# Down matrices of the experts issued from ScalarE's DMA queue in a two-layer decoder step

## The reference, cut to what matters

```python
def expert_block(args):
    xblk, e = args
    hid = jax.nn.silu(xblk @ w_eg[e]) * (xblk @ w_eu[e])
    return hid @ w_ed[e]
```

## Time and profile before

| | us |
|---|---|
| median of 3 runs | 1869.09 |
| lowest and highest | 1864.49, 1871.01 |
| the profiled execution, its own time | 1871.93 |
| its span in the profile | 1870.2 |
| PE busy | 1424.5 |
| DVE busy | 473.6 |
| ACT busy | 323.3 |
| POOL busy | 299.8 |

### The profile page before, as it was taken

How to read it: one execution, slowest core, us unless ns; L and a number is a source line. 1 busy time by engine, 2 the same in 40 slices (tenths; PEclk the granted TensorE clock), 3 DMA queues, 4 the chain that set the end, 5 groups by cost and what they waited for, 6 DMA issues and landing times. The chain is left out here.

```text
span 1870.2 us, 20816 instructions
## 1 busy us (share of the span) xinstructions
PE 1424.5 (76%) x7932; PEld 780.5 (42%) x7932; DVE 473.6 (25%) x1019; ACT 323.3 (17%) x656; POOL 299.8 (16%) x394
## 2 busy tenths in 40 slices
PE   6999655599498777777771799878599877777770
PEld 3554233445254444444440443345355444444440
DVE  1013544532411000000003287822411100000014
ACT  3122221201111000000001143544111000000001
POOL 1000010100111111111110285700012111111110
PEclk9999655598699999999996799978699999999995
DMA  7600000113799999999994800410599999999984
GB/s 210 242 25 1 6 1 3 18 23 45 326 418 419 420 421 420 420 420 420 420 391 153 295 0 1 180 19 12 221 395 418 420 420 420 420 420 420 420 365 156
DMA packets 99025, 478.04 MB, mean 256 GB/s; under 512 B 25463, under 2 KB 28551, under 8 KB 49784
## 3 DMA queue, kind: packets, MB, share of 16 engines
q1 hardware_dynamic: 86040, 452.67, 59.8%
q0 software_dynamic: 12928, 24.62, 4.7%
HBM read 467.50 MB, written 28.27 MB: 265 GB/s over the span
## 5 line engine op out<-in xcount | busy, mean ns | idle before, releaser
L1312 PE MATMUL psum<-ring,arena 128*64 128x256 f32 x4096 | 470.4, 384 | 99.5 <-DMA ring<-in_w_expert_up 57.9
L1312 PEld LDWEIGHTS psum<-ring,arena 128*64 128x64 f32 x4096 | 293.3, 138 | 259.1 <-DMA ring<-in_w_expert_up 79.7
L1333 PE MATMUL psum<-ring,arena 128*64 128x512 f32 x1024 | 238.9, 608 | 77.3 <-issue 75.6
L1436 POOL COPY arena<-arena 128x1 int32 (+1 forms) x122 | 23.2, 190 | 854.2 <-DVE arena L1414 646.1
L1333 PEld LDWEIGHTS psum<-ring,arena 128*64 128x64 f32 x1024 | 79.7, 139 | 192.0 <-issue 188.4
L1414 DVE COPY arena<-psum 128x512 f32<-128x512 f32 x64 | 44.3, 692 | 325.9 <-PE psum L1333 325.9
L1889 PE MATMUL psum<-arena,ring 128*128 128x512 f32 x256 | 114.2, 605 | 8.7 <-DMA ring<-in_w_pw 8.7
L2122 DVE SCALAR_TENSOR_TENSOR psum<-arena,psum 128x512 f32<-128x512 f32 x136 | 102.8, 756 | 16.1 <-PE psum L1903 11.6
L1405 DVE TENSOR_TENSOR arena<-psum,arena 128x256 f32<-128x256 f32 x64 | 27.2, 425 | 306.2 <-ACT arena L1377 306.2
L1830 POOL TENSOR_TENSOR ring<-ring 128x512 f32<-128x512 f32 x72 | 91.6, 1273 | 39.3 <-ACT ring L2024 24.3
L1371 ACT ACTIVATE arena<-psum 128x512 f32<-128x512 f32 x64 | 38.2, 597 | 323.7 <-PE psum L1299 323.7
(11 more groups left out here) (398 smaller groups left out, 1270.0 us busy)
## 6 DMA issues: line engine op xcount, KB each, us to landing
ring<-in_w_expert_gate SPq DMA_DIRECT2D x64, 2048.0 KB, 34.2
ring<-in_w_expert_up SPq DMA_DIRECT2D x64, 2048.0 KB, 34.4
ring<-in_w_expert_down SPq DMA_DIRECT2D x64, 2048.0 KB, 34.5
arena<-y_rows SPq DMA_DIRECT2D x16, 512.0 KB, 6.4
ring<-in_w_pw SPq DMA_DIRECT2D x4, 2048.0 KB, 21.1
ring<-in_w_in_mix SPq DMA_DIRECT2D x3, 2048.0 KB, 20.4
ring<-in_w_out_mix SPq DMA_DIRECT2D x1, 4096.0 KB, 29.1
ring<-in_w_pw SPq DMA_DIRECT2D x1, 4096.0 KB, 25.8
```

The source lines that it names most:

```text
L1312: last = nc.tensor.matmul(P[q * CAP:(q + 1) * CAP, bank, 0:HF], Q["xt"][:, c, h, :], w[:, h, c, q * HF:(q + 1) * HF], start=(h == 0 and c ...
L1333: last = nc.tensor.matmul(P[q * CAP:(q + 1) * CAP, 4, :], Q["hidt"][:, c, h, :], ring(u)[2][:, h, c, q * HB:(q + 1) * HB], start=(h == 0 a ...
```

## The change

SP no longer issues the down matrices of the experts 3 to 31. ACT issues them: behind the copy of turned hidden rows of expert `e` it waits for `y_done` of expert `e - 1` and issues down(e+2). The last round of three experts is taken out of ACT's loop, since the expert 30 has no matrix to issue. Gate and up stay with SP, in their order. The same is done in both layers, and in the code of further passes, which isn't run for these inputs.

```diff
             def sp_rest(self, sp, layer, before):
 
-                def step(e, u):
-                    self.load(sp, layer, e, u, before, True, (0, 1))
-                    self.load(sp, layer, e - 1, (u + 2) % 3, before, True, (2,))
-
                 self.load(sp, layer, 3, 0, before, True, (0, 1))
                 with sp.Fori(0, (NE - 5) // 3) as i:
                     for c in range(3):
-                        step(i * 3 + (4 + c), (1 + c) % 3)
-                step(NE - 1, (NE - 1) % 3)
-                self.load(sp, layer, NE - 1, (NE - 1) % 3, before, True, (2,))
-
+                        self.load(sp, layer, i * 3 + (4 + c), (1 + c) % 3, before, True, (0, 1))
+                self.load(sp, layer, NE - 1, (NE - 1) % 3, before, True, (0, 1))
...
-            def act(self, act, before):
+            def act(self, act, layer, before):
...
                         sigmoid(e)
                         copy_x(e + 1)
                         copy_hid(e)
+                        if isinstance(e, int) and e + 2 >= NE:
+                            continue
+                        self.load(act, layer, e + 2, c, before, True, (2,))
 
                 three(0)
-                with act.Fori(1, (NE - 2) // 3) as i:
+                with act.Fori(1, (NE - 2) // 3 - 1) as i:
                     three(i)
+                three((NE - 2) // 3 - 1)
                 sigmoid(NE - 1)
                 copy_hid(NE - 1)
```

More of the change, by code:

```diff
@@ L1581, in moe_act @@
                 nc.scalar.activation(VAL[:, 1, :, :, 0], Q["oh2"], ACT.Copy, scale=Q["m5"][:, 10, 0:1]).then_inc(RE["vals_made"], 1)
-                main_pass.act(act, 0)
-                more(act, layer, lambda b: more_pass.act(act, b))
+                main_pass.act(act, layer, 0)
+                more(act, layer, lambda b: more_pass.act(act, layer, b))
                 if final:
```

## The result

The changed kernel takes 1888.91 us (median of 5 runs, 1883.37 to 1892.37) against 1871.01 (5 runs, 1864.49 to 1874.81): a ratio of 1.0096, 95% interval 1.0068 to 1.0124. It is slower by 17.9 us; 17.0 were forecast. The profiled execution has a span of 1887.2 us, 17.0 us more than before.

A forecast was written before the change was run, and what follows sets the result against it. The prediction took the DMA engines, full at 420 GB/s, to bound both expert passes. PE's tail after the last landing grows 8.5 us a layer: 1869.1 + 17.0 = 1886.1 us, range 1868 to 1900.

The forecast's parts named there:

- The stream bounds the pass and keeps its length: Both expert passes: busy DMA engines limit them; first issue to last landing stays 461 us in layer 1, at 420 GB/s.
- Nothing is won on SP, nothing lost on ACT: Issue of weights: 29 x 4.31 us a layer saved on SP worth nothing; ACT's added issues covered, 0 us.
- A down matrix shares the engines instead of standing behind SP's backlog: Down loads from ACT's queue: landing about 13 us after issue instead of 34.5.
- Down(31) lands about 9 us before up(31): End of each pass: down(31), issued about 22 us before the end, lands 13 us later; up(31) lands last.
- The tail grows by 8.5 us a layer, 17.0 in all: PE's work after the last landing: 3.60 + 4.91 us more in each layer; chance 0.66.
- the 4.91 us: End of layer 1 on PE: time from start of down(30) to start of down(31), turn and copy included.
- the lower end: Tail after the last landing: 0.4 us may be a wait for down(31), so 8.1 us a layer, 16.2 in all.
- The order of landing stays: Rival, end of pass: down(31) still lands last, tail stays 3.65 us, time 1869 to 1871 us; chance 0.13.
- Faster: Rival, DMA engines: second queue raises the rate; 2.5%, 431 GB/s, would give 1863 us; chance 0.07.
- slower still: Rival, DMA engines: interleaving two queues costs rate, adding 11 to 22 us, 1897 to 1908 us; chance 0.14.

The follow-up runs named there:

- e2: Changed kernel, but down(30) and down(31) issued by SP behind up(31), ACT issuing down only up to expert 29: 1872.04 us against 1867.95 for the kernel before.
- e4: Kernel before, but ACT issues the gate matrices, SP up and down in their old order: 1876.99 us, ratio 1.0043 to the kernel before.
- e1: Kernel before, SP issuing everything, but down(30) and down(31) ahead of gate(31) and up(31): 1888.03 us against 1867.95.
- e6: Kernel with SP issuing down(30), down(31) ahead of gate(31), up(31), plus 56 unused small matmuls ahead of gate(31): 1886.94 us; kernel before 1867.89.

## Why the prediction was right

*The stream bounds the pass and keeps its length.* Right: 460.3 to 461.9 us in layer 1 and 472.0 to 473.2 in layer 0, in all eight kernels, with one queue or two.

*Nothing is won on SP, nothing lost on ACT.* Right: a gate's issue on SP fell from 4.45 to 0.37 us in the median without a gain. ACT's took 0.38 us, and e2 bounds all costs of the second queue at 6.5 us.

*A down matrix shares the engines instead of standing behind SP's backlog.* Right, with 14.8 us in the steady stretch where 13 was worked out. The Trainium skill (DMA: Bandwidth & Descriptors, section Queues, rings and completion order) has a ring for ACT on every engine, served in turn; the new queue q10 and the 14.9 us beside 40 agree. What the Trainium skill says on the same page, section Issuing engines are not separate DMA queues, that issuing from several engines only saves issue time, agrees with the rate here, 420 GB/s both times; the order of landing changed all the same.

*Down(31) lands about 9 us before up(31).* 8 us in layer 0 (962.44 + 14.2 = 976.6 against 984.7), 3.3 in layer 1. There up(29) landed 27.6 us ahead of up(31) instead of 31.8, and down(31) was asked for 17.7 us before the end instead of 22 (the prediction's own items give 23).

*The tail grows by 8.5 us a layer, 17.0 in all.* The mechanism was right. The sum was right in part by luck: its two halves were mis-sized, and the errors nearly cancelled. Layer 1 grew by 11.7 - 3.7 = 8.0 us; the 4.91 us held 0.4 of a wait for down(31), as the lower end supposed (1836.51 to 1841.03 in the timeline after, 4.52). Layer 0 grew by 14.75 - 3.65 = 11.1 us. Its stream was 1.0 us shorter (514.89 to 987.9 before, 512.73 to 984.7 after), that of layer 1 0.9. Together 19.1 - 1.9 = 17.2, against 17.0 in the span. What the prediction left out is PE's backlog and its clock: it took PE to stand waiting for up(31) at full clock, and in layer 0 PE was 3.2 us late to it, 2.7 of them from the matmuls that took 6.38 instead of 3.67 us. That the span agrees so well is luck too: what lies outside the passes differs by 0.1 us in this pair of executions, and by up to 6 us among the eight.

*The rivals.* "The order of landing stays" is refuted by the changed kernel's own chain, and e2, which puts the order at the end back, returns the time. "Faster" and "slower still" both needed another rate than 420 GB/s; there is none.

Open is how much of e4's loss is the clock and how much the faster arrival at the end: its trace gives 3.0 and 2.2 us of PE's delay in layer 1, and no run takes them apart. Waits get longer and rarer with two queues: between 600 and 960 us PE stood 80.7 us in 65 waits of at most 2.0 before, and 63.3 us in 19 waits of up to 6.7 after. Why they do was not tried by itself. No version here beats the kernel before.

## What to carry to other kernels

In this stream, bound by transfers, a second issuing queue changed no rate, but it changed which bytes landed last; look there first in a kernel like it, and let the matrix with the least work behind it be the last one. When loads of one kind arrive early, check at the end of the stream whether the rest then arrives faster than the engine can use it, as in e4: its backlog is as dear as a wait. The long issue times on SP were no cost here, as the DMA engines behind them were full.

## What had not been expected of the hardware

With down or gate matrices on ACT's queue, PE's mean clock in the pass was 0.90 to 0.92 (600 to 960 us; 0.99 with SP alone) at the same rate. PE's idle time came in fewer, longer pieces, as counted above. The granted clock, in two pieces of the changed kernel's layer 1, the wait ahead of up(29) and the first 2.6 us of its matmuls:

```profile
1799.00:1805.40 6.40, 0.10 (x3) 0.01 (x2) 0.42 (x1) 0.38 (x1) 1.04 (x1) 0.69 1.01 420
1805.40:1808.00 2.60, 2.60 (x12) 1.47 (x14) 0.00 (x0) 0.00 (x0) 0.00 (x0) 0.50 1.03 418
```

During the idle 6.3 us the clock fell, and the matmuls began at 0.50, the lower level of 1.2 GHz: 5.08 us instead of 3.67. Inside the stream that is hidden behind the transfers; at its end, on PE's path, it cost up to 3.0 us a layer (e4), and nothing where PE still had to wait for up(31) afterwards, as in layer 1 of the changed kernel. With the wait of 11 us in e1 filled with small matmuls (e6), the matmuls after it ran at full clock and were 2.5 us shorter.
